# Loading expert weights in pieces of 2 MB instead of 1 MB: another rule for which buffer a load takes

## The chip, the cores and the metric

The kernel runs on one core of a Trainium2 chip. The metric is the device time of one execution in microseconds (us). Before the change it is 1584.67 us, the median of three runs (1584.25 to 1585.34).

## The reference

Two transformer blocks are computed one after the other on 256 tokens of width 1024 in 32-bit floats, each with its own kind of attention or recurrence, and each ends in a mixture of experts. The mixtures are what the change touches:

```python
def hier_moe(h, w_rg, b_rg, w_re, b_re, w1, w3, w2):      # first block: 32 experts of width 256
    ...
    top_p, top_i = lax.top_k(jax.nn.softmax(logits_in, axis=-1), TOP_K)
    ...
        hid = jax.nn.silu(jnp.einsum('td,edf->tef', t, w1[sl])) * jnp.einsum('td,edf->tef', t, w3[sl])
        out = out + jnp.einsum('tef,efd->td', hid * gate[:, gi, :, None], w2[sl])

def grouped_moe(x, w_router, b_router, w_gate, w_up, w_down):   # second block: 16 experts of width 1024
    ...
    for e in range(N_EXPERTS_2):
        h = jax.nn.silu(t @ w_gate[e]) * (t @ w_up[e])
        y = y + gate_dense[:, e:e + 1].astype(t.dtype) * (h @ w_down[e])
```

Each token uses two experts. The kernel reads every expert's weights once from memory: 96 MB for the first mixture, 192 MB for the second (1 MB here is 1,048,576 bytes).

## The kernel before

**Stages.** The first block's dense part runs to about 715 us, the first mixture to about 945, the second block's attention to about 1120, the second mixture to about 1570, and a layer norm ends the program.

**How a mixture is tiled.** The weights are cut into slices of 3 MB, each for 256 hidden columns of one expert: 2 MB of up weights (first half and second half of the 1024 input rows, 1 MB each, with both the gate and the up matrix) and 1 MB of down weights. In memory a slice is 128 rows (one for each partition) of 24 KB: 8 KB for the first half of ups, 8 KB for the second half, 8 KB for downs. TensorE works through *steps*. A single step is one slice, a pair step two slices of two experts side by side in TensorE's columns, a quad step four. The first mixture has 11 steps in its order of execution (pair, pair, pair, quad, pair, quad, quad, pair, quad, quad, pair), the second has 32: eight units of four steps, namely pair (steps 0 to 3), pair (4 to 7), single (8 to 11), pair (12 to 15), quad (16 to 19), single (20 to 23), pair (24 to 27), pair (28 to 31).

**Order of work on TensorE (PE) in `mixture`.** For every step t: the ups of step t+1, first halves (`up(t+1, 0)`); the turning of step t's hidden values; at a unit's first step the combine of the last unit and the gather of a later one; the ups of step t+1, second halves (`up(t+1, 1)`); the downs of step t. The matmuls of a first half need only the first halves of the weights.

**Buffers and loads.** Weights arrive in buffers of 8 KB per partition (1 MB). There are 21 of them in a mixture: 11 in `ring` (0 to 10), and ten others that lie in tensors which the stage no longer needs: `x_ctx` (tensor xc), `heads` (o_heads), `masks` (first_w), `head_w`, `squares` and `normed` (hc), `tokens`, `buffers`, `routing` and `places` (arena). Five of the last join late, when a named semaphore says that their tensor is free (`joins` in `slot_table`).

All loads are issued by SyncE (SP), strictly in the order of one list (`mixture_loads(m, True)`): ups of step 0, ups of step 1, downs of step 0, ups of step 2, downs of step 1, and so on. `slot_free` makes SP wait before a load until its buffer is free: TensorE increments `slots_used` with every buffer's last matmul, and SP waits for a number of it, the *use number* of the buffer's last content (`FREE_AT`). As SP is one queue, a load that waits holds back all behind it. `slot_table` gives buffers out first in, first out in the order of the loads, so that with 21 buffers a load waits for the buffer of the load 21 places before. The same list serves the dense weights (`load_dense`, 1 MB each, 16 buffers), whose use numbers are 1 to 56 before the first mixture and 153 to 168 before the second. In the second mixture the use numbers are 169 to 360.

In the text, MB 0 to MB 191 are the megabytes of the second mixture in the order of loading, MB 192 is the table of the last norm (1 MB too). In the kernel before, each of them is one load.

## Time and profile before

| | us |
|---|---|
| median of 3 runs | 1584.67 |
| the profiled execution, its own time | 1583.29 |
| its span in the trace | 1581.6 |
| TensorE busy | 1470.9 (93%) |
| VectorE busy | 509.7 (32%) |
| ScalarE busy | 328.2 (21%) |
| GpSimd busy | 152.0 (10%) |
| moved by DMA | 403.98 MB, mean 255 GB/s |

The page cuts the span into 40 slices of 39.5 us and gives the busy share of each engine in tenths; its DMA line is the mean busy share of the core's 16 DMA engines. A mean over the span hides that these stages have different limits, so the stretches are read by themselves. SPq stands for SP's queue, in which an issue's row gives the moment at which SP issued the load; when SP had waited for a buffer, that is the moment at which the buffer came free.

### The profile page before, as it was taken

Reading aid. Unit: us, or ns where it says so; the run is one execution under the profiler, and the core shown is the slowest. Engines: PE = TensorE matmul, PEld = TensorE weight load, DVE = VectorE, ACT = ScalarE, POOL = GpSimd, SP = SyncE. Lnnn points to the kernel's source line nnn. Section 1 sums busy time; section 2 is a strip of 40 time slices with the busy share of each in tenths; the row PEclk is TensorE's granted clock in tenths of the full one; section 3 lists DMA queues with packets and bytes.
Section 4 is the critical chain, followed back from the end, with each engine's and each line's share of the span. In section 5 each row is a group of like instructions: output and inputs, shape, how many; then the busy total and the mean of one; then the engine's idle time right before and its main releaser. Section 6 shows DMA issues by size and latency. Waiting matters only on the chain.

```text
span 1581.6 us, 21236 instructions
## 1 busy us (share of the span) xinstructions
PE 1470.9 (93%) x8151; PEld 948.8 (60%) x8151; DVE 509.7 (32%) x1074; ACT 328.2 (21%) x722; POOL 152.0 (10%) x170
## 2 busy tenths in 40 slices
PE   6899999999999999999998789999999999569996
PEld 2577777787588888875554359977534443124432
DVE  2567777667630311144221120042511110101002
ACT  2343343433431200021010011161100000000001
POOL 1334433334200000000000000000000000000000
PEclk9999999999999999999999999999999999989999
DMA  9711111111655344547799998405499999999996
GB/s 383 319 54 40 53 40 40 40 40 53 264 214 195 140 153 168 172 160 318 315 423 423 423 421 337 145 16 208 186 424 421 424 402 424 423 424 424 422 421 265
DMA packets 58860, 403.98 MB, mean 255 GB/s; under 512 B 6833, under 2 KB 6961, under 8 KB 12448
## 3 DMA queue, kind: packets, MB, share of 16 engines
q1 hardware_dynamic: 52992, 382.96, 59.9%
q0 software_dynamic: 5792, 19.95, 4.2%
q8 instruction: 54, 0.88, 0.2%
q14 instruction: 22, 0.18, 0.0%
HBM read 401.79 MB, written 1.10 MB: 255 GB/s over the span
## 4 chain that ended last, share of the span: by engine, by line
PE 72%; SPq 11%; DMA 6%; DVE 5%; issue 2%; ACT 2%; POOL 1%; DVEq 0%; ACTq 0%; POOLq 0%
PE bank L695 71%; SPq L525 10%; DMA ring<-in_moe 2%; DMA o_heads<-in_moe 2%; DMA arena<-in_moe 2%; ACT arena L1464 1%; DVE arena L1907 1%; POOL arena L637 1%; PE bank L1159 1%; DMA xc<-in_xc 1%; DMA decay_rows<-arena 0%; SPq L536 0%; DVE arena L1896 0%; DVE arena L1898 0%; ACT hc L1464 0%
## 5 line engine op out<-in xcount | busy, mean ns | idle before, releaser
L695 PE MATMUL bank<-arena 128*128 128x128 f32 (+7 forms) x3112 | 520.0, 338 | 30.8 <-DVE arena L1898 15.1
L695 PEld LDWEIGHTS bank<-arena 128*128 128x128 f32 (+3 forms) x3112 | 380.5, 183 | 181.1 <-issue 95.0
L1464 ACT ACTIVATE arena<-bank 128x256 f32<-128x256 f32 (+2 forms) x373 | 161.2, 447 | 1065.3 <-PE bank L695 794.2
L695 PE MATMUL bank<-ring,arena 128*64 128x512 f32 (+2 forms) x1232 | 339.4, 625 | 39.0 <-DMA ring<-in_moe 17.9
L695 PEld LDWEIGHTS bank<-ring,arena 128*64 128x64 f32 (+2 forms) x1232 | 101.7, 135 | 196.4 <-issue 194.4
L695 PE MATMUL bank<-hc,head_w 128*128 128x512 f32 (+1 forms) x384 | 162.4, 525 | 0.5 <-DVE hc L1831 0.5
L2253 DVE TENSOR_TENSOR arena<-arena,bank 128x256 f32<-128x256 f32 x43 | 18.1, 421 | 332.5 <-ACT arena L1464 332.5
L695 PE MATMUL bank<-hc,arena 128*64 128x512 f32 (+1 forms) x216 | 93.9, 612 | 1.9 <-DMA ring<-in_moe 1.2
L695 PE MATMUL bank<-hc,ring 128*128 128x256 f32 x416 | 91.2, 379 | 0.0
L695 PEld LDWEIGHTS bank<-hc,ring 128*128 128x128 f32 x416 | 78.4, 190 | 11.1 <-issue 0.8
L1464 ACT ACTIVATE arena<-arena 128x512 f32<-128x512 f32 (+4 forms) x139 | 66.0, 507 | 39.9 <-DVE arena L1848 25.4
L1928 DVE TENSOR_TENSOR arena<-bank,first_w 128x512 f32<-128x512 f32 x80 | 55.3, 692 | 55.7 <-PE bank L695 53.4
L695 PEld LDWEIGHTS bank<-hc,head_w 128*128 128x128 f32 x384 | 63.8, 192 | 14.5 <-issue 10.9
L695 PE MATMUL bank<-arena,ring 128*128 128x256 f32 x320 | 70.8, 379 | 1.2 <-DVE arena L2026 1.2
L2247 DVE COPY arena<-bank 128x512 f32<-128x512 f32 x19 | 13.1, 692 | 175.5 <-PE bank L695 175.4
L695 PE MATMUL bank<-head_w,arena 128*128 128x128 f32 (+3 forms) x168 | 62.2, 510 | 6.7 <-DMA ring<-in_moe 5.6
L695 PEld LDWEIGHTS bank<-arena,ring 128*128 128x128 f32 x320 | 60.7, 190 | 9.8 <-DVE arena L2026 1.6
L1846 DVE SCALAR_TENSOR_TENSOR arena<-arena,vec 128x512 f32<-128x512 f32 (+1 forms) x72 | 65.0, 903 | 1.2
L642 POOL TENSOR_TENSOR arena<-arena,first_w 128x512 f32<-128x512 f32 x40 | 54.9, 1372 | 101.8 <-PE bank L695 60.6
L695 PE MATMUL bank<-first_w,arena 128*64 128x512 f32 (+3 forms) x144 | 58.9, 539 | 2.1 <-DVE arena L1902 1.4
L695 PE MATMUL bank<-xc,arena 128*64 128x512 f32 (+2 forms) x112 | 52.3, 610 | 0.0
L695 PE MATMUL bank<-o_heads,arena 128*64 128x512 f32 (+2 forms) x112 | 52.2, 610 | 0.0
(269 smaller groups left out, 1301.5 us busy)
## 6 DMA issues: line engine op xcount, KB each, us to landing
ring<-in_moe SPq DMA_DIRECT2D x154, 1024.0 KB, 23.1
ring<-in_dense SPq DMA_DIRECT2D x59, 1024.0 KB, 9.5
arena<-in_moe SPq DMA_DIRECT2D x51, 1024.0 KB, 24.6
hc<-in_moe SPq DMA_DIRECT2D x27, 1024.0 KB, 22.6
head_w<-in_moe SPq DMA_DIRECT2D x14, 1024.0 KB, 24.4
xc<-in_moe SPq DMA_DIRECT2D x14, 1024.0 KB, 21.1
o_heads<-in_moe SPq DMA_DIRECT2D x14, 1024.0 KB, 20.6
first_w<-in_moe SPq DMA_DIRECT2D x14, 1024.0 KB, 22.5
```

What stands on the lines that cost most here:

```text
L525: sp.dma_start(into, rows_[part % len(rows_)][:, at:at + GROUP]).then_inc(sem_, 16)
L637: nc.gpsimd.tensor_tensor(beta_half[1], beta_half[1], et[1], ALU.mult).then_inc(s["back_half"], 1)
L642: nc.gpsimd.tensor_tensor(levels[k % 2], coupling, times(M(f"off{k}"), TT), ALU.mult).then_inc(s["level_masked"], 1)
L695: return nc.tensor.matmul(out, lhsT, rhs_, start=start, stop=stop, **kw)
L1159: ins = nc.tensor.transpose(bank[4 + step_no % 2][:, f * P:(f + 1) * P], hid[:, f * P:(f + 1) * P], M("ident"))
L1464: return nc.scalar.activation(out, in_, func, **kw)
L1846: link(stt(c3, src, wgt, c3, ALU.mult, ALU.add))
L1907: stt(flat(conv[0]), flat(conv[0]), float(P) ** -0.5, flat(norms[0]), ALU.mult, ALU.mult).then_inc(s["normed"], 1)
L1928: tt_(group_of(picked, g), grown(g), times(M(f"pick{k + 1}"), 4), ALU.mult).then_inc(s["picked"], 1)
L2247: cp(x_cols[u % 2][:, 4:8, :].rearrange("p a b -> p (a b)"), bank[7][:, :]).then_inc(s["x_copied"], 1)
L2253: tt_(hid, act_h, bank[4 + step_no % 2][:, FS:2 * FS], ALU.mult).then_inc(s["hid_ready"], 1)
```

## The change

An expert slice's ups are now loaded by one DMA of 2 MB (`load_up`), 128 rows of 16 KB, into two neighbouring buffers; its downs by one of 1 MB (`load_down`) into a single buffer. Seven pairs of buffers may take ups: five in the ring, (0,1) to (8,9), then (`tokens`, `buffers`) and (`squares`, `normed`). A pair is free when both its buffers are, and an up load keeps both until its second half has been used (`take(..., ("up", m, t, j, 1))`). A load no longer takes the buffer next in a queue: an up takes the pair, a down the single buffer, with the lowest use number; for a down a buffer that belongs to a pair counts as 6 later. The five buffers that join late enter with an assumed use number, and with a real wait for their semaphore, which the load that takes them makes. The loads' order (in experts' slices) is the same, but for a quad or pair step one load now brings first and second half of one expert, where before all first halves came ahead of all second halves. TensorE's matmuls and their order are the same; for its first ups of a step it now waits until both halves of all the step's experts have landed (`up_view`).

```diff
-UP_SLOTS = {"quad": 8, "pair": 4, "single": 2}
-DOWN_SLOTS = {"quad": 4, "pair": 2, "single": 1}
...
+DOUBLE = [(home, home + 1) for home in range(0, RING - 1, 2)] + [("tokens", "buffers"), ("squares", "normed")]
+PAIRED_HOMES = {home for pair in DOUBLE for home in pair}
...
+def mixture_loads(m):
+
+    return [(what, t, j) for what, t in mixture_turns(m, True) for j in range(WIDTH[STEPS[m][t][0]])]
+
+
+def slots_in_order_of_use(m):
+
+    return [(what, m, t, j, part) for what, t in mixture_turns(m, False) for part in range(2 if what == "up" else 1)
+            for j in range(WIDTH[STEPS[m][t][0]])]
...
-    free = [(home, 0) for home in range(RING)]
-    home_of, filled, landed_at, free_at = [], {home: base for home, (_, base) in SHARED_SEMS.items()}, [], []
-    for n in range(len(order)):
-        if n in joins:
-            free.insert(0, (joins[n][0], 0))
-        if n == between:
-            free = [f for f in free if f[0] not in ("tokens", "buffers", "squares", "routing", "places")]
-        home, used = free.pop(0)
...
+    def take(homes, what, last_use):
+        home = homes[0]
         filled[home] = filled.get(home, 0) + 16
...
+        home_of[what], landed_at[what] = home, filled[home]
+        joins[what] = [new.pop(h) for h in homes if h in new]
+        known = [free[h] for h in homes if free[h] == int(free[h])]
+        free_at[what] = int(max(known, default=0))
+        for h in homes:
+            free[h] = float(used[last_use])
+
+    def enter(home, at, sem, value):
+        free[home], new[home] = at, (sem, value)
+
+    def single(apart=()):
+        return min((h for h in free if h not in apart), key=lambda h: free[h] + 6.0 * (h in PAIRED_HOMES))
...
+            enter("tokens", end + 0.1, "out2_made", KT)
+            enter("buffers", end + 0.1, "out2_made", KT)
+            enter("squares", end + 0.2, *("ln_var", 1))
+            enter("routing", end + 0.3, "order_ready", 2)
+            enter("places", end + 0.4, "slot_rows_made", 4)
+        for what, t, j in mixture_loads(m):
+            if what == "up":
+                pair = min(DOUBLE, key=lambda pair: max(free[h] for h in pair))
+                take(list(pair), ("up", m, t, j), ("up", m, t, j, 1))
+            else:
+                take([single()], ("down", m, t, j), ("down", m, t, j, 0))
...
+        apart2 = {"tokens": area(5120, 2 * GROUP), "squares": hc[:, :, :, :].rearrange("p s k n -> p (s k n)")}
...
+        def double_at(what):
+
+            home = HOME[what]
+            return apart2[home] if home in apart2 else ring[:, home:home + 2, :].rearrange("p a n -> p (a n)")
...
-            def load_step(m, kind, what, step_no, part, rows_):
-
-                n = SLOT[what, m, step_no, part]
-                into, sem_ = slot_free(n)
-                at = part // len(rows_) * GROUP + (0 if what == "up" else 2 * KT * FS)
-                sp.dma_start(into, rows_[part % len(rows_)][:, at:at + GROUP]).then_inc(sem_, 16)
+            def load_up(m, step_no, j, row):
+
+                what = ("up", m, step_no, j)
+                sem_ = slot_free(what)
+                sp.dma_start(double_at(what), row[:, 0:2 * GROUP]).then_inc(sem_, 16)
+
+            def load_down(m, step_no, j, row):
+
+                what = ("down", m, step_no, j)
+                sem_ = slot_free(what)
+                sp.dma_start(slot_at(what), row[:, 2 * GROUP:3 * GROUP]).then_inc(sem_, 16)
...
-                def slot_view(what, step_no, part):
-                    n = SLOT[what, m, step_no, part]
-                    pe.wait_ge(landed[HOME[n]], LANDED_AT[n])
-                    return slot_at(n)
+                def up_view(step_no, j, part):
+                    what = ("up", m, step_no, j)
+                    pe.wait_ge(landed[HOME[what]], LANDED_AT[what])
+                    return double_at(what)[:, part * GROUP:(part + 1) * GROUP].rearrange("p (k f) -> p k f", k=4)
...
-                        w = [slot_view("up", step_no, wide * part + j).rearrange("p (k f) -> p k f", k=4) for j in range(wide)]
+                        w = [up_view(step_no, j, part) for j in range(wide)]
```

What SP issues ahead of the second mixture, each row with the tensor that holds the buffer and what it waits for; before:

```order
L525 DMA ring<-in_moe 128x2048 [waits slots_used] x3
L525 DMA hc<-in_moe 128x2048 [waits slots_used]
L525 DMA head_w<-in_moe 128x2048 [waits slots_used]
L525 DMA ring<-in_moe 128x2048 [waits slots_used] x7
L525 DMA xc<-in_moe 128x2048 [waits slots_used]
L525 DMA o_heads<-in_moe 128x2048 [waits slots_used]
L525 DMA first_w<-in_moe 128x2048 [waits slots_used]
L525 DMA ring<-in_moe 128x2048 [waits slots_used]
L525 DMA arena<-in_moe 128x2048 [waits out2_made]
L525 DMA arena<-in_moe 128x2048 [waits xc_squared,out2_made]
L525 DMA hc<-in_moe 128x2048 [waits ln_var]
L525 DMA ring<-in_moe 128x2048 [waits slots_used] x3
```

and now:

```order
L565 DMA ring<-in_moe 128x4096 [waits slots_used] x4
L571 DMA head_w<-in_moe 128x2048 [waits slots_used]
L571 DMA ring<-in_moe 128x2048 [waits slots_used]
L565 DMA ring<-in_moe 128x4096 [waits slots_used]
L565 DMA arena<-in_moe 128x4096 [waits out2_made]
L571 DMA hc<-in_moe 128x2048 [waits slots_used]
L571 DMA xc<-in_moe 128x2048 [waits slots_used]
L571 DMA o_heads<-in_moe 128x2048 [waits slots_used]
L571 DMA first_w<-in_moe 128x2048 [waits slots_used]
L565 DMA ring<-in_moe 128x4096 [waits slots_used] x2
```

The rows `ring 128x4096 x4` are the ups of steps 0 and 1. Before, sixteen loads of 1 MB stood ahead of the first that waits for `out2_made`. Now the second expert's ups of step 2 take that pair (arena, 128x4096): 12 MB stand ahead of it, and behind it the downs of steps 1 and 2 (4 MB in hc, xc, o_heads and first_w).

What SP issues ahead of the first mixture; before:

```order
L525 DMA head_w<-in_moe 128x2048 [waits sgu_taken]
L525 DMA ring<-in_moe 128x2048 [waits slots_used] x7
L525 DMA xc<-in_moe 128x2048 [waits slots_used]
L525 DMA o_heads<-in_moe 128x2048 [waits slots_used]
L525 DMA first_w<-in_moe 128x2048 [waits slots_used]
L525 DMA ring<-in_moe 128x2048 [waits slots_used] x4
L525 DMA arena<-in_moe 128x2048 [waits rest_taken]
L525 DMA arena<-in_moe 128x2048 [waits xc_squared,rest_taken]
L525 DMA hc<-in_moe 128x2048 [waits norm_summed]
```

and now:

```order
L565 DMA ring<-in_moe 128x4096 [waits slots_used] x3
L565 DMA arena<-in_moe 128x4096 [waits rest_taken]
L571 DMA head_w<-in_moe 128x2048 [waits sgu_taken]
L571 DMA ring<-in_moe 128x2048 [waits slots_used]
L565 DMA ring<-in_moe 128x4096 [waits slots_used] x2
L571 DMA xc<-in_moe 128x2048 [waits slots_used]
L571 DMA o_heads<-in_moe 128x2048 [waits slots_used]
L571 DMA first_w<-in_moe 128x2048 [waits slots_used]
L571 DMA arena<-in_moe 128x2048 [waits beta_made,slots_spread]
```

The ups of step 1's second expert now take the pair that waits for `rest_taken`, as fourth load of the mixture; before, that wait stood ahead of the sixteenth. The last row now waits for `slots_spread`, before for `norm_summed`.

The loads of step 16, the first quad step of the second mixture, where TensorE's second half of an earlier step frees the buffers; before, the first six of its eight loads of ups:

```order
L525 ISA [waits slots_used]
L525 DMA ring<-in_moe 128x2048
L525 ISA [waits slots_used]
L525 DMA ring<-in_moe 128x2048
L525 ISA [waits slots_used]
L525 DMA ring<-in_moe 128x2048
L525 ISA [waits slots_used]
L525 DMA hc<-in_moe 128x2048
L525 ISA [waits slots_used]
L525 DMA arena<-in_moe 128x2048
L525 ISA [waits slots_used]
L525 DMA arena<-in_moe 128x2048
```

and now all four:

```order
L565 ISA [waits slots_used]
L565 DMA ring<-in_moe 128x4096
L565 ISA [waits slots_used]
L565 DMA arena<-in_moe 128x4096
L565 ISA [waits slots_used]
L565 DMA ring<-in_moe 128x4096
L565 ISA [waits slots_used]
L565 DMA ring<-in_moe 128x4096
```

The wait of each is a number of `slots_used` that the rows don't show. Both versions of `slot_table` give them; here for the loads that the text speaks of (a number in brackets says whose buffer it was):

```
second mixture                  before: buffer, use waited for     now: buffer(s), use waited for
ups of step 0                   1, 2, 3, normed: 153 to 156        (4,5): 155   (8,9): 157
ups of step 1                   head_w, 4, 5, 6: 157 to 160        (0,1): 162   (2,3): 164
ups of step 2                   9, 10, x_ctx, heads: 163 to 166    (6,7): 168   tokens: out2_made
ups of step 3 (MB 18 to 21)     squares: ln_var; 1, 2, 3: 169-171  (4,5): 171   (8,9): 172
ups of step 4 (from MB 22)      normed: 172                        (0,1): 175 (second half of step 1)
ups of step 14, MB 72           220                                (8,9): 226 (second half of step 11)
ups of step 15, MB 76           224                                (0,1): 230 (second half of step 12)
ups of step 16, MB 82           230                                (6,7): 235 (second half of step 13)
ups of step 16, MB 86           234 (and MB 87: 235)               (4,5): 241 (second half of step 14)
downs of step 15                238, 239                           head_w: 224, ring 10: 227
first mixture
ups of step 4, second expert    64, 65                             (0,1): 69 (second half of step 2)
ups of step 5, second expert    72, then 81 (downs of step 2)      squares: 77 (second half of step 3)
```

Use 241 and the others are the same matmul in both versions. In the trace of the kernel before, a use number's moment is seen where SP had waited for it: use 155 at 966.57 us, 157 at 981.85, 162 at 1016.62, 164 at 1076.67, 168 at 1096.53, 169 at 1128.75, 171 at 1132.18, 175 at 1145.21, 226 at 1270.36, 230 at 1281.35, 235 at 1299.49, 241 at 1310.33; in the first mixture 69 at 755.88 and 81 at 777.43. These are the issues of the loads whose `FREE_AT` is that number.

## Rows read from the trace of the kernel before

**Rows 1.** The page: busy tenths in 40 slices of TensorE and of DMA.

```profile
PE   6899999999999999999998789999999999569996
...
DMA  9711111111655344547799998405499999999996
```

**Rows 2.** Windows of the mixtures: us, busy of each engine, PEclk, DMA share, GB/s.

```profile
722.00:766.00 44.00, 44.00 (x261) 24.72 (x260) 13.37 (x32) 4.91 (x10) 0.00 (x0) 1.00 1.01 423
766.00:779.00 13.00, 13.00 (x93) 6.73 (x93) 4.30 (x10) 1.58 (x3) 0.00 (x0) 1.00 0.28 103
779.00:942.00 163.00, 141.85 (x916) 76.44 (x913) 30.88 (x70) 17.95 (x37) 0.00 (x0) 0.96 1.01 422
1108.00:1130.00 22.00, 19.76 (x103) 13.66 (x104) 15.14 (x70) 4.50 (x7) 0.00 (x0) 0.84 0.03 6
1130.00:1131.00 1.00, 1.00 (x8) 0.29 (x4) 0.90 (x6) 0.00 (x0) 0.00 (x0) 1.00 0.60 205
1131.00:1296.00 165.00, 165.00 (x694) 69.75 (x692) 21.10 (x50) 14.14 (x33) 0.00 (x0) 1.00 1.01 423
1296.00:1301.00 5.00, 5.00 (x26) 1.71 (x24) 1.59 (x5) 0.38 (x1) 0.00 (x0) 1.00 0.78 279
1301.00:1563.00 262.00, 230.28 (x1134) 86.48 (x1130) 20.50 (x47) 17.98 (x43) 0.00 (x0) 0.97 1.01 423
```

**Rows 3.** The chain that ended last, 1480 to 1582 us: start, us, what.

```profile
1537.22 26.86 DMA arena<-in_moe
...
1564.22 3.67 PE bank L695 x16
```

**Rows 4.** TensorE's waits, 1340 to 1582 us: total us, times, longest.

```profile
PE bank L695 <- DMA ring<-in_moe: 16.2, 5, 5.9
```

**Rows 5.** SP's timeline, 950 to 1146 us: start, us, issue.

```profile
981.85 0.33 SPq L525 DMA_DIRECT2D head_w<-in_moe  x1
...
1096.53 0.33 SPq L525 DMA_DIRECT2D ring<-in_moe  x1
1096.90 0.91 SPq L525 DMA_DIRECT2D arena<-in_moe  x2
...
1132.18 0.33 SPq L525 DMA_DIRECT2D ring<-in_moe  x1
...
1145.21 0.34 SPq L525 DMA_DIRECT2D ring<-in_moe  x1
```

**Rows 6.** SP's timeline of single issues, 1076 to 1311 us.

```profile
1076.67 0.33 SPq L525 DMA_DIRECT2D ring<-in_moe  x1
1128.75 3.76 SPq L525 DMA_DIRECT2D ring<-in_moe  x3
1270.36 0.33 SPq L525 DMA_DIRECT2D ring<-in_moe  x1
1281.35 0.34 SPq L525 DMA_DIRECT2D ring<-in_moe  x1
1299.49 0.33 SPq L525 DMA_DIRECT2D arena<-in_moe  x1
1310.33 0.33 SPq L525 DMA_DIRECT2D ring<-in_moe  x1
```

**Rows 7.** SP's timeline in the first mixture.

```profile
691.25 0.42 SPq L525 DMA_DIRECT2D arena<-in_moe  x1
755.88 0.33 SPq L525 DMA_DIRECT2D ring<-in_moe  x1
777.43 0.33 SPq L525 DMA_DIRECT2D arena<-in_moe  x1
```

**Rows 8.** DMA by queue: 4 to 8 us (rows of 16 KB), then 1200 to 1250 us.

```profile
q1 hardware_dynamic: 98, 1.61, 95.0%
...
q1 hardware_dynamic: 2893, 21.10, 101.0%
```

**Rows 9.** DMA issues, 1076 to 1097 us: KB each, median us to landing.

```profile
ring<-in_moe SPq DMA_DIRECT2D x2, 1024.0 KB, 4.8
```

145 lines of the change are left out of this document (77 added, 68 removed).

## Prediction

> **What bounds the kernel now.** I read the page's slices first, then windows of the two mixtures, then the end of the chain, and last SP's queue. In the slices DMA stands at 9 where the mixtures run, twice, and low between them [rows 1]. The windows give the rate: in the second mixture DMA is at 1.01 and 423 GB/s from 1131 to 1296 us and from 1301 to 1563, in the first from 722 to 766 and from 779 to 942 [rows 2]. So one load of 1,048,576 bytes takes 1.0486 / 0.423 = 2.479 us in a stream. TensorE is busy in all of 1131 to 1296, but only 230 of 262 us after it, and what it waits for there is loads: 16.2 us in five waits on the ring alone [rows 2, 4]. The chain ends with a DMA of 26.86 us that has landed at 1564.08, and TensorE follows at 1564.22 [rows 3]. The end is therefore set by the moment at which the last of the second mixture's loads has gone through, and that is: where the stream starts, plus 2.479 us for each load, plus every hole in it.
>
> There are two holes in the second mixture before. The first is 1108 to 1130 (share 0.03): 19 loads are in (MB 0 to 18), and SP waits for the first matmuls to free a buffer; it issues MB 19 at 1128.75, and since the engines are busy 0.60 of 1130 to 1131 the stream starts at 1130.4, about 1.6 us after the issue [rows 2, 6]. The second is 1 us long, in 1296 to 1301 (0.78): MB 87 is issued at 1299.49 and goes at 1301.1. As a check: 106 loads are left then (MB 87 to 192), 1301.1 + 106 x 2.479 = 1563.9, and the chain says 1564.08. So before, the buffers only just suffice to let DMA run ahead while TensorE does the single steps, for which it needs fewer bytes.
>
> **The change, part by part.** TensorE's matmuls are the same, in the same order, and up to 1340 us nothing but its own work holds it in the second mixture. So a use number can't come earlier than before, and for each load of the new list I take the moment of the use that it waits for, from SP's rows, add 1.6 us, and compare with where the old stream stood then.
>
> *Ahead of the second mixture.* Now the ups of steps 0 and 1 wait for uses 155 to 164, the last at 1076.67 [rows 6], and 10 MB can be in before 1096.53. At 1096.53 and 1096.90 [rows 5] the ups of step 2 and four downs follow: 8 MB from 1098.1, gone at 1117.9. SP then stands before MB 18, which wants a whole pair, and the first such pair is free at use 171, the second half of step 0's ups: 1132.18 instead of 1128.75 [rows 5, 6]. Stream at 1133.8. The old stream stood at 19 + (1133.8 - 1130.4) / 2.479 = 20.4 then: 2.4 MB behind. Four MB go until 1143.7, and the ups of step 4 want use 175, at 1145.21 [rows 5], so stream at 1146.8 with MB 22, where the old one stood at 25.6: 3.6 MB behind, 9.0 us.
>
> *The single steps.* With 14 of 21 buffers in pairs that are let go only at a second half, while the downs' buffers stand empty behind a waiting up (the downs of step 15 could go since use 224), DMA can run less far ahead. MB 72 waits for use 226, 1270.36: stream at 1272.0, the old one at 76.1, so 4.1 MB behind. MB 76: 1281.35, at 1283.0 the old one at 80.6, 4.6 behind. MB 82 waits for use 235, 1299.49, which before was MB 87's wait: 5 behind. MB 86 waits for use 241, 1310.33 [rows 6]: stream at 1311.9, the old one at 87 + 10.8 / 2.479 = 91.4, 5.4 MB behind, 13.3 us. The gaps don't add: each gives the place of the stream anew, and the last decides. From there DMA falls behind TensorE's need and buffers come free ahead of SP, in quads too: step 17's last pair needs use 255, in step 16's second half, which at TensorE's old pace comes at about 1340, and the stream comes to it at 1311.9 + 12 x 2.479 = 1341.6. That is the closest of them.
>
> *Rows of 16 KB.* The old trace has one load with such rows, xc's at the start. In 4 to 8 us q1 moved 1.61 MB at a share of 95.0%: 0.4237 MB per busy us. From 1200 to 1250, rows of 8 KB, it is 21.10 / (1.010 x 50) = 0.4178 [rows 8]. So 16 KB rows are 1.4% better; I take that, with 0 and 2.2% as bounds (1.61 is rounded, and neighbouring windows differ). Of the 107 MB from MB 86 on, 68 are ups: 68 x 2.479 x 1.4% = 2.4 us (0 to 3.7). Before MB 86 it gives nothing, since uses set the place there. The Trainium skill, *DMA: Bandwidth & Descriptors*, section *Why small descriptors are slow (HBM only)*, has about 3 cycles of overhead for each packet of 32-byte beats. By that 8 KB costs 259 cycles and 16 KB 515, 0.6% less per byte, an estimate that would make the term 1.0 us instead of 2.4; the row is nearer 1.4%, on a small sample.
>
> Second mixture: last landing at 1311.9 + 107 x 2.479 - 2.4 = 1574.8 against 1563.9, +10.9 us. The tail after it is the same work.
>
> *The first mixture.* Step 1's second pair now waits for `rest_taken`, 691.25 [rows 7], as the fourth load, and 11 MB go from 692.9 to 720.2; TensorE begins the mixture only at about 714 and needs step 1's ups after step 0's, so this costs nothing. Then the second expert's ups of step 4 (MB 28 of this mixture) want use 69, at 755.88 [rows 7], not 65: stream at 757.5, when the old one stood at 18 + (757.5 - 721.8) / 2.479 = 32.4. But the old one then has a hole until 779.1, as MB 37 waits for the downs of step 2 (777.43; share 0.28 in the window) [rows 2, 7], and the new list has no such wait: eight MB bring it to MB 36 at 777.3, 0.3 MB behind at 779.1, 0.7 us. In the quads it must wait for second halves that themselves wait for eight landed MB; for step 9's third pair the stream and the use come out about together, so I take 1.7 us, half of a half step (3.4 us, as uses 169 and 171 are apart [rows 5, 6]). Less 1.4% of 38 MB of ups, 1.3 us: +1.1 in all, bounds -2 and +5, since here TensorE's own times move. The stretch between the mixtures is TensorE's and moves with it.
>
> *TensorE.* That a quad's first half now waits for 8 MB instead of 4 shows as longer waits, but DMA sets the pace there. It costs only if it lets DMA run dry (in the bounds of the first mixture).
>
> Sum: 10.9 + 1.1 = +12.0 us on the profiled execution's 1583.29, 1595.3. The runs' median is 1.4 above that execution, so I say 1596.5.
>
> **Rivals.**
> *The larger rows win (faster).* If the new lists kept DMA as busy as before, only the rate would count: of about 433 us of saturated second mixture and 167 of the first (207 less 16 dense loads) [rows 2], two thirds are ups, 400 x 1.4% = 5.6 us less: 1579. It decides if no load waits longer than before. For it: SP often waits before and DMA hardly shows it. Against: use 241 can't come before 1310.3, and the old stream was 4 MB past MB 86 by then. The same side is taken by the Trainium skill's *DMA: Bandwidth & Descriptors*, *Measured (HBM→SBUF, 128 partitions, SWDGE, issued from GpSimd)*, where 1 MB moves at 341 GB/s and 16 MB at 425, so fewer, larger DMAs would gain much; here a lone load lands 4.8 us after its issue [rows 9], but in a stream it takes 2.479, so its fixed part is hidden already and the trace disagrees. 6 in 100, of which that page's rule in this kernel 1.
>
> *Only the hole at the start stays.* If the single steps ran without a wait, 3.6 MB or 9.0 us would remain, less 1.4% of 113 MB of ups, 3.9: +5.1, with the first mixture +6.2, 1591. For it: DMA comes late and so has free buffers for a while. Against: MB 82 and 86, by their use numbers. 10 in 100.
>
> *The quads run dry as well.* If pairs let go late leave DMA idle for 1 to 2 us in each of the nine quad steps, or TensorE, after stalls of 10 us where 5.9 was the longest on the ring [rows 4], works at a lower clock (0.96 and 0.97 in the windows with stalls, 1.00 in those without [rows 2]) at the mixture's last steps, 5 to 10 us come on top: 1602 to 1606. 14 in 100.
>
> *It cancels.* Rows of 16 KB at their upper bound and a first mixture 2 us better bring it back only in part; no change needs the start hole gone too. 4 in 100.
>
> **How the numbers follow.** The forecast has 66 in 100, with 1592 to 1601 as its own range. The 80% range reaches to the start-only case and into the dry quads: 1589 to 1603. A measurement of this kernel can tell 0.2%, 3.2 us. Slower by more: 66 + 10 + 14 = 90 in 100; within: 4; faster: 6.
>
> **What would show it.** Right: DMA idle from about 1118 to 1134 with a short hole at 1144 to 1147; share below 1 in 1265 to 1312, above all just before 1301 and 1312; rows of 16 KB at 427 to 430 GB/s in the later stretches; last landing about 1575 (plus the first mixture's shift); TensorE's longest waits near 10 us, at first halves of quads; the hole of 766 to 779 gone and one near 752 to 757 in its place. Wrong: MB 86 (step 16's third pair, two neighbours of the ring) issued before 1309, or DMA without a hole before 1312; then the faster rival holds. A share well below 1 after 1320 is the dry-quads rival.

## The result, and the profile after

The changed kernel takes 1606.47 us (median of 4 runs, 1604.87 to 1607.46), the kernel before, run beside it, 1585.01 (1584.25 to 1589.15). The ratio is 1.0129, with a 95% interval of 1.0109 to 1.0149: slower by about 21 us. The direction was forecast, the size wasn't: 1596.5 with a range up to 1603. The profiled executions are 1604.87 and 1583.29 us, 21.6 apart, and the mean granted clock fell from 0.983 to 0.971.

The page of the changed kernel, its slices (40.1 us each), answers to [rows 1]:

```profile
PE   6899999999999999999987799999999996759996
...
PEclk9999999999999999999998999999999998879999
DMA  9711111111854434437999896106599999999995
```

DMA now has an 8 in slice 23 (882 to 922 us), inside the first mixture, where it had 9s, and TensorE two 7s there; shares of 0.90 in the second mixture still read 9. Windows of the changed kernel place this (columns as in [rows 2]):

```profile
730.00:766.00 36.00, 36.00 (x215) 19.25 (x212) 9.69 (x23) 4.31 (x9) 0.00 (x0) 1.00 0.86 358
766.00:880.00 114.00, 97.23 (x648) 52.63 (x647) 21.41 (x50) 9.82 (x20) 0.00 (x0) 0.91 1.01 428
880.00:888.00 8.00, 8.00 (x68) 4.54 (x68) 1.25 (x3) 0.98 (x2) 0.00 (x0) 1.00 0.26 109
...
1117.00:1131.00 14.00, 12.62 (x61) 9.78 (x61) 9.14 (x47) 2.62 (x5) 0.00 (x0) 0.76 0.72 301
1131.00:1276.00 145.00, 144.15 (x623) 60.83 (x623) 26.22 (x74) 13.16 (x29) 0.00 (x0) 1.00 0.91 383
1276.00:1323.00 47.00, 47.00 (x202) 19.02 (x202) 5.56 (x13) 4.04 (x10) 0.00 (x0) 1.00 0.90 359
1323.00:1572.00 249.00, 206.66 (x1022) 78.09 (x1018) 17.87 (x40) 16.47 (x39) 0.00 (x0) 0.91 1.01 427
```

The hole of 766 to 779 us is gone. In its place stand a loss in 730 to 766 (0.14 x 36 = 5.0 us) and a hole in 880 to 888 (0.74 x 8 = 5.9 us), which the kernel before doesn't have. In the second mixture DMA is at 0.91 and 0.90 up to 1323, where it was 1.01 with one hole of 1 us, and at 1.01 from there on.

To split the loss I use one instruction that stands between the mixtures: the last start in TensorE's group bank<-one_row,ones, a small matmul in the second mixture's routing ("the router row" from here on). The group in the kernel before, then in the changed kernel (duration min/median/max ns, first and last start us):

```profile
L695 PE MATMUL bank<-one_row,ones x8: 249/266/295, 693.8 to 1105.4; 1*128 1x36 f32 x4, 1*128 1x16 f32 x4
```

```profile
L744 PE MATMUL bank<-one_row,ones x8: 249/266/295, 694.5 to 1114.4; 1*128 1x36 f32 x4, 1*128 1x16 f32 x4
```

The first start, in the routing ahead of the first mixture, is 0.7 us late already; I have no cause for that (it stands at 694.0 to 694.8 in all the runs below). The last is 9.0 us late, so the first mixture and what follows it cost 8.3. From there to the end it was 1583.29 - 1105.4 = 477.9 us and is 490.5: 12.6 more. SP's timeline of the changed kernel shows that the shift of 9.0 stays as it is while TensorE sets the pace. The uses that came at 1270.36, 1281.35, 1299.49 and 1310.33 [rows 6] now let SP go at 1279.3 (the second of the two issues of the first row), 1290.32, 1308.52 and 1319.32:

```profile
1268.83 10.85 SPq L565 DMA_DIRECT2D ring<-in_moe  x2
...
1290.32 0.86 SPq L565 DMA_DIRECT2D ring<-in_moe  x2
...
1308.52 0.34 SPq L565 DMA_DIRECT2D ring<-in_moe  x1
...
1319.32 0.87 SPq L565 DMA_DIRECT2D ring<-in_moe  x2
```

The end of the chain, which answers to [rows 3]:

```profile
1543.96 29.78 DMA arena<-in_moe
1573.75 0.14 issue
1573.88 3.65 PE bank L744 x16
1577.54 0.37 PE bank L1213 x2
1577.90 7.02 PE bank L744 x32
...
1585.76 3.71 PE bank L744 x16
```

The last up weights land at 1573.75, both halves at once, and four downs follow them. The last of these is issued at 1549.39 and lands 34.9 us later, at 1584.3. Before, TensorE took the last downs 0.14 us after their landing; here it is still busy with the last two half steps and comes to them at 1585.76, 1.5 us after it. So the loads are 20.2 us late at the end (1584.3 for 1564.08), and TensorE adds 1.3.

TensorE's waits from 1340 us on, which answer to [rows 4] (total us, times, longest):

```profile
PE bank L744 <- DMA ring<-in_moe: 25.4, 4, 12.9
PE bank L744 <- DMA arena<-in_moe: 17.5, 2, 15.9
```

And the place of the hole at 880, on TensorE's timeline (start, us, what, in brackets the idle time before it and what ended it), then on SP's:

```profile
857.79 0.59 PE L744 MATMUL bank<-ring,arena 128*32 128x512 f32 x1
869.45 1.03 PE L744 MATMUL bank<-ring,arena 128*32 128x512 f32 x1 [11.07 <-DMA ring<-in_moe]
869.46 1.06 PE L744 MATMUL bank<-arena 128*32 128x512 f32 x1
...
883.24 0.62 PE L744 MATMUL bank<-ring,arena 128*32 128x512 f32 x1
```

```profile
887.03 0.33 SPq L565 DMA_DIRECT2D ring<-in_moe  x1
```

Step 8's first half waits 11.07 us until all eight of its megabytes are in, then runs at 1.06 us a matmul instead of 0.59 (6.4 us instead of 3.7; the granted clock is 0.56 in 869 to 876, about the lower level, after 11 us without work), its second half begins at 883.24, and only its end, use 125, lets SP load the third pair of step 9. SP issues nothing between 856 and 887.03, and DMA runs dry from 880 on.

The same half in the kernel before, and the downs of step 9:

```profile
857.99 1.03 PE L695 MATMUL bank<-ring,arena 128*32 128x512 f32 x1 [6.17 <-DMA ring<-in_moe]
...
922.42 0.62 PE L695 MATMUL bank<-ring,arena 128*32 128x512 f32 x2 [3.44 <-DMA o_heads<-in_moe]
```

and in the changed kernel the first half and the downs of step 9:

```profile
899.70 1.03 PE L744 MATMUL bank<-hc,arena 128*32 128x512 f32 x1 [9.24 <-DMA arena<-in_moe]
...
931.38 0.62 PE L744 MATMUL bank<-o_heads,arena 128*32 128x512 f32 x1
```

Before, step 8's first half began when four of its megabytes were in; it ran at the lower clock too (5.9 us, granted clock 0.62 in 858 to 864), and the second half began at 871.20. So use 125 comes 12 us later now: 9.9 for four more megabytes (4 x 2.479), 1.5 because the loads were that much later, and only 0.6 because the half at the lower clock is a little longer.

How late the loads are along the first mixture follows from each load's issue and its time to landing. The 76th megabyte lands at 877.8 before and 879.1 now, 1.3 us later; the 80th at 887.6 and 894.7, 7.1 later; the last at 927.3 and 935.0, 7.8 later. So the hole costs 5.8. TensorE itself is 9.0 late at the downs of step 9: before, it had waited for them and began 0.1 us after they landed; now it began the first half of step 9 at 899.70, after waiting 9.24 us for all eight megabytes, had its own work from there, with one wait of 1.29 us for a load, and came to the downs 1.2 us after their landing (930.1). From the end of this mixture to the router row the two kernels take the same 160.3 us.

### The profile page after: what moved, and what is told of

Its sections match the earlier page's. It is cut to its first block, busy times and chain, and to the rows that moved or that the text cites. A ratio compares the mean times of both kernels' runs of the same rounds, so it can differ in the third digit from the quotient of the medians.

```text
span 1603.2 us, 20976 instructions
## 1 busy us (share of the span) xinstructions
PE 1473.0 (92%) x8151; PEld 949.5 (59%) x8151; DVE 509.6 (32%) x1074; ACT 328.5 (20%) x722; POOL 152.3 (9%) x170
## 4 chain that ended last, share of the span: by engine, by line
PE 78%; DMA 11%; DVE 5%; issue 2%; ACT 2%; POOL 1%; SPq 1%; DVEq 0%; ACTq 0%; POOLq 0%
PE bank L744 76%; DMA ring<-in_moe 7%; DMA arena<-in_moe 2%; ACT arena L1518 1%; DMA xc<-in_moe 1%; DVE arena L1961 1%; PE bank L1213 1%; SPq L571 1%; POOL arena L686 1%; DMA xc<-in_xc 1%; DVE arena L1950 0%; DVE arena L1952 0%; DMA decay_rows<-arena 0%; DVE arena L1955 0%; DVE arena L1956 0%
## 5 line engine op out<-in xcount | busy, mean ns | idle before, releaser
L744 PE MATMUL bank<-arena 128*128 128x128 f32 (+6 forms) x3136 | 567.3, 340 | 36.9 <-DVE arena L1952 15.1
L744 PEld LDWEIGHTS bank<-arena 128*128 128x128 f32 (+3 forms) x3136 | 390.9, 183 | 174.9 <-issue 88.5
L744 PE MATMUL bank<-ring,arena 128*64 128x512 f32 (+2 forms) x1304 | 373.9, 628 | 51.6 <-DMA ring<-in_moe 32.2
L744 PEld LDWEIGHTS bank<-ring,arena 128*64 128x64 f32 (+2 forms) x1304 | 111.4, 137 | 213.3 <-issue 209.0
L744 PE MATMUL bank<-hc,arena 128*32 128x512 f32 (+2 forms) x184 | 89.7, 634 | 9.2 <-DMA arena<-in_moe 9.2
L744 PEld LDWEIGHTS bank<-hc,ring 128*128 128x128 f32 x416 | 78.4, 190 | 11.1 <-issue 0.8
L744 PE MATMUL bank<-arena,ring 128*128 128x256 f32 x352 | 78.0, 379 | 1.2 <-DVE arena L2080 1.2
L744 PEld LDWEIGHTS bank<-hc,head_w 128*128 128x128 f32 x384 | 63.8, 192 | 14.5 <-issue 10.9
L744 PE MATMUL bank<-head_w,arena 128*128 128x128 f32 (+3 forms) x152 | 53.3, 489 | 2.6 <-DMA ring<-in_moe 2.6
L744 PE MATMUL bank<-first_w,arena 128*64 128x512 f32 (+3 forms) x128 | 49.9, 517 | 1.4 <-DVE arena L1956 1.4
L744 PEld LDWEIGHTS bank<-hc,arena 128*32 128x32 f32 (+2 forms) x184 | 24.2, 138 | 40.3 <-issue 40.0
L744 PE MATMUL bank<-xc,arena 128*64 128x512 f32 (+1 forms) x96 | 44.9, 613 | 0.0
## 6 DMA issues: line engine op xcount, KB each, us to landing
ring<-in_dense SPq DMA_DIRECT2D x59, 1024.0 KB, 10.9
ring<-in_moe SPq DMA_DIRECT2D x19, 1024.0 KB, 26.6
```

Of the source, the lines that this page charges most:

```text
L744: return nc.tensor.matmul(out, lhsT, rhs_, start=start, stop=stop, **kw)
```

## The experiments

Twelve kernels in three groups of four, each with the kernel before beside it (medians 1586.03 for a, b, d and e, 1584.31 for f, c, h_warm and i, 1585.90 for the rest). Columns: median, ratio to the kernel before with its interval, and of the profiled execution the time, the router row, and the stretch from there to the end.

| run | median us | ratio [95%] | profiled | router row | from there |
|---|---|---|---|---|---|
| before | 1585.01 | | 1583.29 | 1105.4 | 477.9 |
| the changed kernel | 1606.47 | 1.0129 [1.0109, 1.0149] | 1604.87 | 1114.4 | 490.5 |
| a_first | 1592.45 | 1.0043 [1.0026, 1.0060] | 1592.68 | 1112.7 | 480.0 |
| b_second | 1592.79 | 1.0044 [1.0027, 1.0061] | 1593.05 | 1107.7 | 485.4 |
| d_halves_paired | 1612.59 | 1.0168 [1.0151, 1.0185] | 1612.97 | 1117.6 | 495.4 |
| e_soonest | 1577.54 | 0.9951 [0.9934, 0.9967] | 1576.30 | 1099.7 | 476.6 |
| f_soonest_experts | 1576.16 | 0.9949 [0.9932, 0.9966] | 1575.83 | 1097.3 | 478.5 |
| c_pairs_1mb | 1602.91 | 1.0116 [1.0099, 1.0132] | 1602.73 | 1110.8 | 491.9 |
| h_warm | 1609.06 | 1.0156 [1.0139, 1.0173] | 1607.74 | 1118.4 | 489.3 |
| i_pair_kept | 1598.93 | 1.0093 [1.0077, 1.0110] | 1598.20 | 1113.1 | 485.1 |
| j_pairs_kept_both | 1593.47 | 1.0047 [1.0030, 1.0064] | 1593.52 | 1109.7 | 483.8 |
| h2_warm12 | 1603.16 | 1.0107 [1.0091, 1.0124] | 1604.46 | 1113.7 | 490.8 |
| g_four_fewer | 1590.94 | 1.0032 [1.0021, 1.0044] | 1591.05 | 1096.6 | 494.5 |
| k_mixed | 1582.57 | 0.9975 [0.9966, 0.9985] | 1583.20 | 1100.8 | 482.4 |

How far a router row can be trusted: b_second has the loads of the kernel before up to there and is 2.3 us later, g_four_fewer has those of f_soonest_experts and is 0.7 sooner. Differences under 2.5 us in that column tell nothing. Of the 2.3, 1.7 have a source: in the kernel before the downs of step 9 run in 3.7 us behind their wait of 3.44 us, at a granted clock of 1.00; in b_second they wait 3.41 us and take 5.3, at 0.68.

### Which mixture

```diff
-MODE = ("double", "double")     # the changed list and rules in both mixtures
+MODE = ("double", "fifo")       # a_first; "fifo" is the list and the turn of the kernel before
+MODE = ("fifo", "double")       # b_second
```

> The change in the first mixture alone; the second mixture loads as in the kernel before (1 MB halves, buffers in a fixed turn). Theory (the first mixture costs far more than the +1.1 us forecast, because the third and fourth pair of one quad step come late, that step's loads stop the stream, and TensorE starts it cold): everything behind the first mixture is 8 to 9.5 us later than before and nothing more is added, so the profiled run is 1591.5 to 1593.5 us, 8 to 10 over before; DMA share of 850 to 900 us at .88 to .90 again. Rival 1 (the forecast's own term): at most 5 us over before. Rival 2 (the lateness of the first mixture and that of the second are one and the same: buffers freed late in the one are lent to the other): the full 21 us, about 1605, or nothing.

> The change in the second mixture alone; the first loads as in the kernel before. Theory (the second mixture costs what the forecast said of its stream, 10.9, and besides 1.5 to 2.5 us at the end, where the last step's two halves land together): issue of the load that waits for use 241 at 1310.3 plus 0 to 0.7, profiled run 1594.5 to 1597.0 us, 11.5 to 13.5 over before, DMA share below 1 in 1120 to 1150 and 1260 to 1320 us as in the changed kernel (less its shift of 9). Rival (the second mixture suffers since the first runs late): under 1590. With a_first: the two differences add up to 20 to 23 us if the parts are independent.

Measured: a_first is 9.4 us over the kernel before by the profiled executions (6.4 by medians), 7.3 of it at the router row. The time is in the theory's range, but at the router row stand 7.3 where it said 8 to 9.5, and 2.1 come behind it, where nothing was to be added. The forecast's own term (at most 5) falls all the same. b_second is a miss of the theory: 9.8 by the profile, of which only 7.5 lie behind the router row, where 12.6 were to come. By medians the two come to 6.4 + 6.8 = 13 us, and the change as a whole to 21. Of the 8 that are in neither part alone, 5 stand behind the router row (12.6 against 7.5); the rest isn't clear of the scatter. A reason for the 5 stands in the two plans of buffers: with the changed rules in both mixtures the dense weights between them lie in other buffers, and in the second mixture the neighbours squares and normed take five single down weights up to step 14 and no up pair before step 17. In b_second they carry up weights from step 2 on. The changed kernel's penalty for a down weight in a paired buffer is 6 uses; when a paired buffer has been free for longer than that, the plan breaks the pair.

### Rule, order, pairs, size of the load: four steps from the one kernel to the other

e_soonest takes the kernel before and changes only the rule; f_soonest_experts also the order; c_pairs_1mb also the pairs; the changed kernel also the size of a load. With the pairs, c_pairs_1mb takes over the rest of the changed plan too: the 6 uses by which a down avoids a paired buffer, and the assumed use numbers of the buffers that join late.

```diff
-return min(free, key=lambda h: stamp[h])                 # the turn of the kernel before
+return min(free, key=lambda h: (free[h], stamp[h]))      # e_soonest and f_soonest_experts
...
-out += [(what, t, j, part) for part in range(2) for j in range(wide)]      # before and e_soonest
+out += [(what, t, j, part) for j in range(wide) for part in range(2)]      # f_soonest_experts and c_pairs_1mb
...
+pair = min(DOUBLE, key=lambda pair: max(free[h] for h in pair))            # c_pairs_1mb, 1 MB into each of the two
```

> 1 MB loads in the order of the kernel before, each with its own buffer and its own release; of the change only the rule stays that a load takes the buffer that was used up first. Theory (the rule costs nothing by itself, the pairs do): not slower than before; the hole of 766 to 779 us, where a load waited for a buffer whose turn it was, closes, and the time falls by 0 to 9 us: 1574 to 1583.5 profiled. Rival 1 (the rule scatters the buffers so that a later load waits for a late use, and is itself a cause of the loss): 3 us or more over before. Rival 2 (the first mixture ends by TensorE's work whatever the loads do): within 1.5 us of before, with the hole closed.

> As e_soonest (1 MB loads, each with a buffer and a release of its own, the buffer used up first), but in the changed kernel's order: both halves of an expert one behind the other, expert by expert, so that TensorE's first half of a quad step waits for the seventh of its eight loads and not for the fourth. Theory (the pairs cost the time, the order little): 0 to 5 us over e_soonest, 1576 to 1582 us profiled, so at or below the kernel before. Rival (the order is the cost: TensorE starts each step later, ends it later, and buffers come free later): 10 us or more over e_soonest, 1587 us or more, with TensorE's waits at quads' first halves up to 7.4 us (three loads of 2.48) longer each.

> The changed kernel with one thing undone: each 2 MB load is issued as two loads of 1 MB with rows of 8 KB into the same pair, in the same place of the order, and TensorE waits for each. Pairs are taken and given back as in the changed kernel. Theory (buffers that come free only two at a time cost the time): within 3 us of the changed kernel, 1603 to 1610 us profiled; the rate falls from 426 to 423 GB/s (2 us lost) and the last step's tail is won back (1.3 us). It lies 22 us or more over f_soonest_experts, which differs by the pairs alone. Rival (the 2 MB DMA is the cost, as its 16 KB rows land late for TensorE): 1595 us or less.

The theories of all three hold to within 0.5 us of their ranges. The rule alone makes the kernel faster, by 8.5 us (0.9951). The order adds nothing (0.9949 against 0.9951), though the first half of a quad now waits for the seventh load and not for the fourth: the rival of the order falls. The pairs, with the changed plan around them, cost 1602.91 - 1576.16 = 26.8 us, 13.5 of them at the router row and 13.4 behind it. How much of this is the plan's rule for downs, a section below shows. The larger loads are 3.6 us more by medians of different groups, 0.0013 in ratios whose intervals overlap: no difference that these runs can show, and none in the sense that the faster rows should have given. Windows of f_soonest_experts, then of c_pairs_1mb, show what the pairs do to the first mixture:

```profile
714.00:730.00 16.00, 14.91 (x82) 7.29 (x82) 12.36 (x38) 1.29 (x3) 0.00 (x0) 1.00 0.49 194
730.00:766.00 36.00, 36.00 (x216) 19.50 (x213) 9.24 (x22) 4.30 (x9) 0.00 (x0) 1.00 1.01 423
766.00:880.00 114.00, 104.62 (x722) 56.71 (x720) 25.72 (x60) 11.38 (x23) 0.00 (x0) 0.97 1.01 423
880.00:888.00 8.00, 7.12 (x42) 3.09 (x43) 0.00 (x0) 0.38 (x1) 0.00 (x0) 0.79 1.01 420
```

```profile
714.00:730.00 16.00, 14.91 (x84) 7.70 (x84) 12.30 (x40) 1.92 (x3) 0.00 (x0) 1.00 0.32 105
730.00:766.00 36.00, 36.00 (x215) 19.15 (x212) 9.83 (x23) 4.30 (x9) 0.00 (x0) 1.00 0.87 355
766.00:880.00 114.00, 97.01 (x673) 55.09 (x672) 21.41 (x50) 10.40 (x21) 0.00 (x0) 0.96 1.01 423
880.00:888.00 8.00, 7.84 (x55) 2.50 (x53) 3.69 (x10) 0.47 (x2) 0.00 (x0) 1.00 0.77 288
```

Without pairs DMA has no hole from 730 on; the one of the kernel before at 766 came from the fixed turn of the buffers (e_soonest, which changes that alone, has a share of 1.01 in 766 to 779).

### TensorE's wait for both halves

```diff
-out += [(what, t, j, part) for j in range(wide) for part in range(2)]      # c_pairs_1mb
+out += [(what, t, j, part) for part in range(2) for j in range(wide)]      # d_halves_paired, the same pairs
```

> Pairs are taken and given back as in the changed kernel, but each expert's up weights come as two loads of 1 MB with rows of 8 KB, all first halves of a step ahead of its second halves, and TensorE waits for each half by itself. Theory (what costs is that a pair comes free only when both its buffers are used, and not the size of the DMA nor TensorE's wait for both halves): still 15 to 28 us over before; the last step's tail is as before (TensorE starts the last down weights on landing, so 1.5 to 2.5 us won there), rows of 8 KB cost 0.7% in the loading stretches (2 to 3 us lost), and the fourth pair of a quad is wanted three loads earlier in the stream than in the changed kernel (up to 7.4 us lost where the pairs are what is waited for). Rival (TensorE's wait for both halves makes uses late, and so buffers): at most 8 us over before, and TensorE's waits at the quads' first halves shorter than in the changed kernel by 5 us or more each. Rival 2 (the 2 MB DMAs themselves do the harm, as a larger piece holds the queues): at most 3 us over before.

29.7 us over the kernel before by the profiled executions (26.6 by medians), 6 us over the changed one. TensorE again starts when first halves are in: from 1340 us on its longest wait for a load is 6.3 us, where it was 15.9. Yet nothing is won, so both rivals fall. The run doesn't price that wait by itself, since the same edit asks for the pairs earlier, and that this costs more than the shorter waits win is the likely reading, not a shown one. The bound of the theory (28) was a little low for the profiled execution.

### How many buffers pairs are worth

```diff
+for home in (7, 8, 9, 10):      # in the second mixture
+    free.pop(home)
```

> f_soonest_experts with four of its buffers (7 to 10 of the ring) left out in the second mixture: from its tenth megabyte on nearly each load waits for a use that is four later. How many buffers is the pairing worth? The second mixture from its router row to the end took 478.5 us in f_soonest_experts and 491.9 in c_pairs_1mb, which differs by the pairs alone. Theory (pairs cost because a buffer used in a step's first half lies idle until the second half of its own expert is used, and then waits for its neighbour: for quads that is up to four buffers held without need): 8 to 20 us more than f_soonest_experts in that stretch, 13.4 if pairs are worth four buffers. Rival (buffers are not what the second mixture is short of, and the pairs cost through something else): under 4 us more.

494.5 us behind the router row, 16.0 more than f_soonest_experts. The pairs cost 13.4 there, as the changed kernel plans them, so they act like some three to four buffers fewer of 21 in that mixture.

### Down weights kept out of the pairs

```diff
-key=lambda h: free[h] + 6.0 * (h in PAIRED_HOMES)
+key=lambda h: free[h] + 60.0 * (h in PAIRED_HOMES)   # i: in the second mixture; j: in both
```

> The changed kernel, but in the second mixture down weights never take a buffer of a pair while a single one will come free (the penalty on a paired buffer raised from 6 uses to 60). In the changed kernel the second mixture's down weights of steps 1, 4, 6, 11 and 14 sit in the pair squares and normed, which so serves no up load until step 17; in b_second, where the dense weights behind the first mixture left the buffers in another turn, that pair carried up loads from step 2 on, and its second mixture cost 7.5 us and not 12.6. Theory (the sixth pair is the difference of 5 us, why a_first and b_second add up to 14 and not 21): 3 to 6 us faster than the changed kernel, 1599 to 1602 us profiled; the holes of 1276 to 1291 us go. Rival (those 5 us come from the first mixture's end running into the second's start, so from lateness and not from buffers): within 1 us of the changed kernel.

> As i_pair_kept, but in both mixtures: down weights stay out of the paired buffers while a single one will come free. In the changed kernel's first mixture the down weights of steps 6, 7 and 9 sit in buffers 6 and 7, so that this pair carries no up load between step 5 and the end, and the third pair of step 9 has to wait for use 125, the second half of step 8; with the pair kept it waits for use 116. Theory (the first mixture's loss of 8.3 us was mis-sized because it rests on one such broken pair, which the hole of 880 to 888 us shows): that hole goes, the second mixture's router row (1114.4 us in the changed kernel, 1113.1 in i_pair_kept) comes 4 to 8 us sooner, and the time is 4 to 8 us under i_pair_kept, 1590 to 1594.5 us profiled; still 14 us or more over f_soonest_experts, which takes any buffers. Rival (the hole only moves, since six pairs do not reach over two quad steps): within 2 us of i_pair_kept.

i_pair_kept: 485.1 us behind the router row instead of 490.5, 6.7 us off the profiled time; the windows of the second mixture, first the changed kernel's and then i_pair_kept's:

```profile
1131.00:1275.00 144.00, 143.15 (x620) 60.35 (x620) 26.22 (x74) 12.93 (x28) 0.00 (x0) 1.00 0.91 383
1275.00:1322.00 47.00, 47.00 (x202) 19.09 (x202) 5.56 (x13) 4.27 (x10) 0.00 (x0) 1.00 0.90 357
```

```profile
1131.00:1275.00 144.00, 143.15 (x613) 59.62 (x612) 25.36 (x69) 12.48 (x28) 0.00 (x0) 1.00 0.94 397
1275.00:1322.00 47.00, 47.00 (x203) 18.88 (x203) 5.56 (x13) 3.88 (x9) 0.00 (x0) 1.00 0.95 391
```

These are the 5 us behind the router row that a_first and b_second didn't add up to (b_second has 485.4 there): the theory of the extra pair holds, a little above its 3 to 6 us, and the rival falls. The expectation calls it the sixth pair; by the plan it is the seventh of seven. j_pairs_kept_both takes 4.7 us more off the profiled time (5.5 by medians), 3.4 of it at the router row (4.7 against the changed kernel). Its windows:

```profile
866.00:880.00 14.00, 9.51 (x51) 4.80 (x51) 0.00 (x0) 0.38 (x1) 0.00 (x0) 0.68 1.01 428
880.00:888.00 8.00, 8.00 (x69) 4.82 (x69) 0.83 (x2) 0.98 (x2) 0.00 (x0) 1.00 0.98 414
```

In 880 to 888 the share is 0.98 where it was 0.26, and the third pair of step 9 is no longer the load that waits there. 3.4 is below the 4 to 8 that I had set against i_pair_kept, and near the scatter of that column. The landings settle it: in j_pairs_kept_both the 76th megabyte of the first mixture lands 1.1 us later than in the changed kernel (880.1), the 80th 4.8 us sooner (889.9), the last 4.7 sooner (930.4). So the hole is gone, and its 5.8 us with it. What is left, 10 us over the kernel before and 17 over f_soonest_experts, is what pairs cost while all seven are whole, together with the loads of 2 MB and TensorE's wait for them. So about 10 of the 27 us above are the rule that lets downs break pairs, and not pairing itself.

### The half clock behind TensorE's long wait

```diff
+if m == 0 and step_no == 7:
+    for _ in range(20):      # h2_warm12: 12
+        mm(bank[4 + (step_no + 1) % 2], ones, times(M("ident"), 4))
 up(step_no + 1, 0)
```

> The changed kernel with 20 matmuls more (ones by the unit matrix, into the bank that the next matmul overwrites) in the first mixture, in front of the first half of step 8, where TensorE waited 11.07 us and then ran the half at 1.06 us a matmul and not 0.59: they fill some 8.6 us of the wait. Theory (2.7 us of the first mixture's loss is the half clock behind that wait: 6.4 us for the half and not 3.7, in which the third pair of step 9 isn't given back): the half runs in 3.7 us again, the hole of 880 to 888 us shrinks by 2 to 3.5 us, the second mixture's router row (1114.4 us in the changed kernel) comes 1.5 to 3.5 us sooner and the time falls by as much. Rival (the slower half is covered, since the loads behind it wait for the second half of step 8, which itself waits for data): the hole and the router row stay within 1 us.

> The changed kernel with 12 matmuls in front of the first half of step 8 of the first mixture, where h_warm had 20: those took 0.87 us each, ran to 875.9 us and pushed the half from 869.45 to 876.23, which made the second mixture's router row 4.0 us late, as much as the half's own end (879.9 for 875.9 us). Twelve take 10.4 us of the 11.07 us of wait. Theory (TensorE's end of step 8 decides when the third pair of step 9 is loaded, us for us, and the half clock makes it 2.7 us late): router row 1.5 to 3.5 us sooner than 1114.4, time 1 to 4 us under the changed kernel. Rival (the half clock is covered, and h_warm's 4.0 us are of another cause): router row within 1 us of 1114.4.

h_warm failed as an experiment: its matmuls are each two instructions of 0.44 us and ran past the landing. Their row, then that of h2_warm12:

```profile
858.86 17.43 PE L744 MATMUL bank<-first_w,ones 128*128 128x512 f32 x40
```

```profile
861.05 10.57 PE L744 MATMUL bank<-first_w,ones 128*128 128x512 f32 x24
```

In both the half then ran in 3.7 us, at full clock. In h2_warm12 the loads were already late when the half became possible, which they owe to the stretch ahead of the edit: the last megabyte that the half needs lands at 871.0 and not 869.3, and the half's end lay at 875.1 and not 875.9 us. By the router row, 0.7 us sooner, the result is the rival's. The dependence shows more clearly in SP's queue: half ends of 875.9, 879.8 and 875.1 us go with issues of step 9's third pair at 887.03, 890.98 and 886.31, some 11.1 us behind each, and with router rows of 1114.4, 1118.4 and 1113.7. And the hole did shrink: between the landings of the 76th and the 80th megabyte lie 15.6 us in the changed kernel and 12.9 in h2_warm12 (880.8 and 893.7). So the lower clock is worth 2.7 us of the hole in the changed kernel. It isn't what the change added, though, as in the kernel before the same half ran at the lower clock too.

### Larger loads where the pair costs nothing

```diff
+if max(free[h] for h in pair) <= sorted(free.values())[1]:
+    take(list(pair), ("up", m, t, j), ("up", m, t, j, 1))                   # one load of 2 MB
+else:
+    for part in range(2):
+        take([soonest()], ("up", m, t, j, part), ("up", m, t, j, part))     # two loads of 1 MB
```

> As f_soonest_experts, but an expert's two halves come in one 2 MB load with rows of 16 KB where a neighbouring pair is free no later than the two buffers used up first would be: 35 of 106 experts, 25 of them in the second mixture; the others as two loads of 1 MB. Estimate: rows of 16 KB moved 1.1% faster (430 for 423 GB/s in stretches of up weights alone), so 35 loads of 4.96 us save 1.9 us where DMA is the bound, and some downs take another buffer that comes free a use or two later. Theory: 0 to 2 us under f_soonest_experts, 1574 to 1576 us profiled. Rival (a 2 MB load holds up the smaller ones behind it, or a use or two of lateness costs more than the rows win): 2 us or more over it.

A miss: 4 us over f_soonest_experts by the ratios and 6.4 by medians; in the profiled executions 3.5 at the router row and 3.9 behind it. The rate rose from 423 to 425 GB/s in 1300 to 1550 us, and the uses that loads wait for moved back by one or two in places. The plan also differs from f_soonest_experts in that a down avoids a paired buffer by one use, and in when the late buffers join. Which load pays for it I haven't traced. What the run shows is that this mix, with its faster rows, is slower than loads of 1 MB alone; that lateness of a use is the reason isn't shown.

## Why the prediction was right in sign and wrong in size

*The second mixture, +10.9.* From the router row to the end it is 12.6, of which 1.3 are the tail, so 11.2 for the stream (20.2 us at the last landing, less the 9.0). The uses at 171, 226, 235 and 241 were the ones that held the loads, and 241 decided, in that order and at the forecast times plus 9.0. This part was right in its mechanism. As the forecast was made from the changed plan itself, the broken pair was in it, though I hadn't seen that it was one: of the 11.2, five came from it. The check of the stream counted MB 192, while the landing at 1564.08 is MB 191's; the slip of one load is in both sums and leaves their difference as it is.

*The tail, "the same work".* Wrong by 1.3 us. Both halves of the last step land together, and TensorE has two half steps and a turn to do before the last downs.

*The first mixture, +1.1, bounds -2 and +5.* This is the step that failed: 8.3 were measured, with 0.7 from ahead of it. The term gave the hole before step 9's third pair 1.7 us, "the stream and the use come out about together", which set use 125 at TensorE's old pace. It is 5.9 us (880 to 888), since that use is in the second half of step 8, which began 12 us later than before: its first half had waited 11.07 us for eight megabytes where it used to need four, with no load issued meanwhile. The prediction had said of TensorE's longer waits that they cost "only if they let DMA run dry", and then left them out of the one place where loads stood right behind them. The plan shares in it: with no pair broken by downs (j_pairs_kept_both) the third pair of step 9 needs only use 116, and the hole is gone. With 5.9 for 1.7 the term would be +5.3. Of the other 3 us, 1.2 are TensorE's own work behind the last loads, the same tail as at the program's end, which the term left out here too. Of the remaining 1.8, the loads lose 0.7 after the 80th megabyte; no run shows the cause, and it is below the scatter of 2.3.

*Rows of 16 KB, 1.4%.* 427 GB/s against 423 over 1323 to 1572, in which 64% are ups: 0.9% on the mix, about 1.5% on the ups. The rate was right and worth the 2.4 us that the sum has. The 0.6% worked out by the Trainium skill's *DMA: Bandwidth & Descriptors*, *Why small descriptors are slow (HBM only)*, lies below what is measured. What a mix of faster rows is worth to the end is another matter: c_pairs_1mb, without them, isn't slower.

*The rivals.* "The quads run dry as well" had 14 in 100 and 1602 to 1606. It was near in its time and in kind (one dry quad and a low clock: 0.91 and 0.56 in windows with waits), but in the first mixture, not the second, where the share after 1323 is 1.01. "The larger rows win" took one true thing: a load that takes the buffer used up first wins 8.5 us, without the larger rows. That the hole of 766 to 779 us was worth so much I had put down as a set-off inside the first mixture only.

*The signs.* DMA stood nearly idle (share 0.13) from 1125 to 1140 us and at 0.62 from 1150 to 1157, where 1118 to 1134 and 1144 to 1147 were forecast on times 9 us earlier; it had a share below 1 up to 1323 and then was full; TensorE's longest waits were 12.9 and 15.9 us at quads' first halves; SP's row of 755.88 is at 757.44. These were right, but for the waits, which were to be near 10 us, and none of them could show the first mixture's size.

## What to carry to other kernels

Where buffers are what lets DMA run ahead, join loads only if the joined buffers also come free together: here a piece twice as large, given back at its second half, cost 27 us as it was planned first and some 17 with every pair kept whole, against about 2 us for the better rate. In the second mixture the first plan cost what three to four of 21 buffers would. Changing the order in which free buffers are taken costs nothing and is worth a try by itself: the earliest-free buffer instead of a fixed turn gave 0.5%, and f_soonest_experts, at 1576 us, is the best version seen. When a forecast moves a wait to "the use of a step", work out when that step can itself begin under the new list, and look in the plan for single users of joint buffers.

## What the chip showed that I had not expected

After 11.07 us without matmuls TensorE ran the next half step at 1.06 us a matmul instead of 0.59, the lower of its two levels (1.2 GHz; the granted clock is 0.56 over 869 to 876 us), where h2_warm12, with matmuls of no use in front, shows 1.00 in the same window. Much shorter waits can go either way: behind 3.44 us without matmuls the kernel before ran the downs of step 9 at a granted clock of 1.00, behind 3.41 us b_second ran the same ones at 0.68 and took 5.3 us for 3.7. Two DMAs of 1 MB and one of 2 MB into the same pair gave times 0.1% apart, within the error. The rules of the first mixture moved the second by 5 us only through which buffers they left free: its matmuls and the order of its loads were the same in b_second and in the changed kernel.
